# High products first, then low products, within each piece of a slab

## The reference

```
proj = x @ w_in                       # mixer layers, 2048 -> 4928
q = (rmsnorm(q_lat, q_norm_g) @ w_uq) ; kv = (rmsnorm(kv_lat, kv_norm_g) @ w_ukv)
y = pool_mixer(...) * silu(g_pool)    # small 128x128 products per group
out = mix @ w_out + b_out ; x = layernorm(DEEPNORM_ALPHA * x + out, ln_g, ln_b)
...
x = x + 0.5 * swiglu(rms_norm(x, ffn1_norm), ffn1_gate, ffn1_up, ffn1_down)   # 2048 -> 5632 -> 2048
proj = rms_norm(x, mix_norm) @ w_in ; x = x + mixed @ w_out
x = x + 0.5 * swiglu(rms_norm(x, ffn2_norm), ffn2_gate, ffn2_up, ffn2_down)
```

## Time and profile before

| | us |
|---|---|
| median of 3 runs | 2,604.45 |
| the profiled execution | 2,607.27 |
| its span | 2,605.5 |
| TensorE busy | 2,571.5 |
| VectorE busy | 1,784.4 |
| ScalarE busy | 1,360.1 |
| granted TensorE clock, mean | 0.998 |

### The profile page before, as it was taken

The page is one execution under the profiler, slowest core; times in us unless marked ns, Lnnn a source line. Parts: engine busy times, 40 slices in busy tenths (PEclk is TensorE's granted clock), DMA queues, the critical chain, the costliest instruction groups (busy, mean ns, idle before and its releaser), DMA issues.

```text
span 2605.5 us, 39929 instructions
## 1 busy us (share of the span) xinstructions
PE 2571.5 (99%) x14246; PEld 2221.6 (85%) x14246; DVE 1784.4 (68%) x2739; ACT 1360.1 (52%) x2112; POOL 0.2 (0%) x4
## 2 busy tenths in 40 slices
PE   7999999999999999999999999999999999999999
PEld 6888888888888888888888887887888888888888
DVE  8777657777658766556666765677776665666655
ACT  6665565565457444444445544774544444444443
POOL 0000000000000000000000000000000000000000
PEclk9999999999999999999999999999999999999999
DMA  7554555454554554565554653444455555555454
GB/s 281 196 184 170 186 210 222 152 187 164 182 209 167 200 184 179 183 202 192 190 193 158 198 210 137 149 152 148 177 195 190 193 168 191 205 193 187 172 186 164
DMA packets 75435, 482.41 MB, mean 185 GB/s; under 512 B 8384, under 2 KB 10816, under 8 KB 30784
## 3 DMA queue, kind: packets, MB, share of 16 engines
q1 hardware_dynamic: 75328, 480.99, 52.2%
HBM read 477.81 MB, written 2.10 MB: 184 GB/s over the span
## 4 chain that ended last, share of the span: by engine, by line
PE 82%; DVE 1%; ACT 1%; issue 0%; ACTq 0%; DVEq 0%
PE acc L800 46%; PE acc L801 23%; PE acc L806 3%; PE acc L808 3%; PE acc L807 3%; PE score L1063 1%; DVE low L1479 0%; PE head_ps L1086 0%; PE turn_ps L1072 0%; ACT high L1142 0%; PE score L800 0%; PE sums L1043 0%; PE head_ps L1087 0%; PE sums L1009 0%; ACT L1421 0%
## 5 line engine op out<-in xcount | busy, mean ns | idle before, releaser
L800 PE MATMUL acc<-xs,high 128*128 128x512 f32 x4096 | 1437.7, 397 | 3.5 <-DVE lat L1589 2.0
L1479 DVE TENSOR_TENSOR low<-raw,high 128x1024 fp32r<-128x1024 f32 (+2 forms) x976 | 1079.4, 1123 | 466.9 <-ACT high L1142 441.2
L1142 ACT ACTIVATE high<-raw 128x1024 fp32r<-128x1024 f32 (+2 forms) x976 | 946.3, 976 | 527.3 <-PE acc L801 382.9
L801 PE MATMUL acc<-xs,low 128*128 128x256 f32 x4096 | 1139.4, 278 | 0.0
L800 PEld LDWEIGHTS acc<-xs,high 128*128 128x128 f32 x4096 | 769.2, 188 | 185.0 <-DVE lat L1589 3.0
L801 PEld LDWEIGHTS acc<-xs,low 128*128 128x128 f32 x4096 | 770.9, 188 | 0.6
L800 PE MATMUL acc<-hidden,high 128*128 128x512 f32 x1408 | 488.9, 394 | 0.1
L1181 ACT ACTIVATE lowsum<-acc 128x256 f32<-128x256 f32 x356 | 136.0, 383 | 532.6 <-PE acc L801 532.3
L801 PE MATMUL acc<-hidden,low 128*128 128x256 f32 x1408 | 390.2, 277 | 0.0
L800 PEld LDWEIGHTS acc<-hidden,high 128*128 128x128 f32 x1408 | 264.0, 188 | 61.8 <-DVE low L1479 0.4
L801 PEld LDWEIGHTS acc<-hidden,low 128*128 128x128 f32 x1408 | 264.3, 188 | 0.0
(11 more groups left out here) (361 smaller groups left out, 1904.0 us busy)
## 6 DMA issues: line engine op xcount, KB each, us to landing
raw<-w_up_dram SPq DMA_DIRECT2D x176, 1024.0 KB, 4.8
raw<-w_down_dram SPq DMA_DIRECT2D x128, 704.0 KB, 4.1
raw<-w_in_dram SPq DMA_DIRECT2D x78, 1024.0 KB, 4.8
raw<-w_out_dram SPq DMA_DIRECT2D x32, 1024.0 KB, 4.8
raw<-w_heads_dram SPq DMA_DIRECT2D x24, 1024.0 KB, 4.8
raw<-w_mixout_dram SPq DMA_DIRECT2D x16, 1024.0 KB, 4.8
raw<-w_mem_dram SPq DMA_DIRECT2D x8, 1024.0 KB, 4.7
raw<-w_nat_dram SPq DMA_DIRECT2D x8, 1024.0 KB, 4.8
```

Of the source, the lines that this page charges most:

```text
L800: eng.matmul(bank_, hi, moving, start=start, stop=False)
L801: return eng.matmul(bank_[:, S:2 * S], lo, moving[:, 0:S], start=False, stop=stop)
L1142: eng.activation(high[:, s % SPLIT, to:to + n * P], raw[:, s % RAW, at_:at_ + n * P], ACT.Copy).then_inc((highs_a, highs_b)[piece], 1)
L1479: eng.tensor_tensor(low[:, s % SPLIT, w], raw[:, s % RAW, at_:at_ + n * P], high[:, s % SPLIT, w].bitcast(F32), ALU.subtract).then_inc((lo ...
```

## The change

In each piece of a slab the high products of all its blocks are issued first, then the low products of all its blocks; before, each block had its high and its low product in turn. The wait for the piece's low part stands before the first low product, and a new wait for its high part stands before the first high one. In the three regions that start with two tiles together (other than `mixout`), the order per block is high of tile 0, high of tile 1, low of tile 0, low of tile 1. In `mixout` it is by piece and tile. In `uq` and `uk` it is by output group (4 or 2 blocks).

The core of the diff:

```diff
-            def product(bank_, hi, lo, moving, start, stop):
+            def product_high(bank_, hi, moving, start):
 
                 eng.matmul(bank_, hi, moving, start=start, stop=False)
+
+            def product_low(bank_, lo, moving, stop):
+
                 return eng.matmul(bank_[:, S:2 * S], lo, moving[:, 0:S], start=False, stop=stop)
...
+                def piece_high(piece):
+
+                    eng.wait_ge((highs_a, highs_b)[piece], val(s + 1, 4, i))
...
+                    cuts = [(b, b + 1) for b in range(KT)] if r.name != "mixout" else [(0, 8), (8, KT)]
+                    for cut, n in [(cut, n) for cut in cuts for n in range(2)] if r.name == "mixout" else [(c, None) for c in cuts]:
+                        tiles = range(2) if n is None else (n,)
+                        for b in range(*cut):
...
+                            for m in tiles:
+                                product_high(banks[m], high[:, (s + m) % SPLIT, at_], in_mix(r)[:, b, :], b == 0)
+                        for b in range(*cut):
+                            at_ = slice(b * P, (b + 1) * P)
                             if b % 8 == 0:
+                                eng.wait_ge((lows_a, lows_b)[b // 8], s + tiles[-1] + 1)
+                            for m in tiles:
+                                last = product_low(banks[m], low[:, (s + m) % SPLIT, at_], in_mix(r)[:, b, :], b == KT - 1)
...
                 elif r.kind == "tile":
                     a = bank_free(k, 4)
-                    for b in range(KT):
-                        if b == 8:
+                    for piece in range(2):
+                        if piece:
                             for step in halfway:
                                 do(*step)
-                        if b % 8 == 0:
-                            piece_ready(b // 8)
-                        if k == 0 and split_norm(r.name):
-                            wait_split(eng, split_norm(r.name), b)
-                        last = product(a, *hl(b), in_mix(r)[:, b, :], b == 0, b == KT - 1)
-                        if b % 8 == 7:
-                            last.then_inc(products, 1)
+                        piece_high(piece)
+                        for b in range(8 * piece, 8 * piece + 8):
+                            if k == 0 and split_norm(r.name):
+                                wait_split(eng, split_norm(r.name), b)
+                            product_high(a, hl(b)[0], in_mix(r)[:, b, :], b == 0)
+                        piece_ready(piece)
+                        for b in range(8 * piece, 8 * piece + 8):
+                            last = product_low(a, hl(b)[1], in_mix(r)[:, b, :], b == KT - 1)
+                        last.then_inc(products, 1)
...
```

More of the change, by code:

```diff
@@ L861, in slot @@
                     banks = bank_free(0, 4), bank_free(1, 4)
[L862 to L874, removed]
-                            if b % 8 == 0:
-                                eng.wait_ge((lows_a, lows_b)[b // 8], s + n + 1)
-                        elif n == 0:
-                            wait_split(eng, split_norm(r.name), b)
-                            if b % 8 == 0:
[L880 to L887, removed]
-                            last.then_inc(products, 1)
@@ new lines, in slot @@
+                    cuts = [(b, b + 1) for b in range(KT)] if r.name != "mixout" else [(0, 8), (8, KT)]
[3 more added lines that the diff above has]
+                            at_ = slice(b * P, (b + 1) * P)
+                            if r.name == "in_a0" and b in (4, 8):
+                                turn_chunk("emb", b // 4 + 1)
+                            if r.name == "mixout":
+                                for step in steps if n == 0 else []:
+                                    if b == (LAST_TURNS[step[1] - MLA_ALL] if step[0] == "turn" else 8):
+                                        do(*step)
+                                if b % 4 == 0 and n == 0:
+                                    eng.wait_ge(mix_l, 4 * DEPTH + b // 4 + 1)
+                                if b % 8 == 0:
+                                    eng.wait_ge((highs_a, highs_b)[b // 8], s + n + 1)
+                            else:
+                                wait_split(eng, split_norm(r.name), b)
+                                if b % 8 == 0:
+                                    eng.wait_ge((highs_a, highs_b)[b // 8], s + 2)
+                            for m in tiles:
+                                product_high(banks[m], high[:, (s + m) % SPLIT, at_], in_mix(r)[:, b, :], b == 0)
+                        for b in range(*cut):
+                            at_ = slice(b * P, (b + 1) * P)
+                            if b % 8 == 0:
+                                eng.wait_ge((lows_a, lows_b)[b // 8], s + tiles[-1] + 1)
+                            for m in tiles:
+                                last = product_low(banks[m], low[:, (s + m) % SPLIT, at_], in_mix(r)[:, b, :], b == KT - 1)
+                                if m:
+                                    if b == KT - 1:
+                                        last.then_inc(products, 2)
+                                elif b % 8 == 7:
+                                    last.then_inc(products, 1)
@@ L906, in slot @@
                     a = bank_free(k // 2, 2) if not half else acc_of(r, r.t0 + k // 2)
[L907 to L913, removed]
+                    for piece in range(2):
+                        cut = (range(0, r.pieces[0]), range(r.pieces[0], HALF))[piece]
+                        piece_high(piece)
+                        for b in cut:
+                            product_high(a, hl(b)[0], hidden[:, HALF * half + b, :], half == 0 and b == 0)
+                        piece_ready(piece)
+                        for b in cut:
+                            last = product_low(a, hl(b)[1], hidden[:, HALF * half + b, :], half == 1 and b == HALF - 1)
+                        last.then_inc(products, 1)
                 elif r.kind in ("uq", "uk"):
@@ L919, in slot @@
                         a = bank_free(k * r.groups + m, 0)
+                        new = m * per in (0, r.pieces[0])
+                        if new:
+                            piece_high(int(m > 0))
                         for b in range(per):
-                            if m * per + b in (0, r.pieces[0]):
-                                piece_ready(int(m * per + b > 0))
-                            last = product(a, *hl(m * per + b), lats[:, src + b, :], b == 0, b == per - 1)
+                            product_high(a, hl(m * per + b)[0], lats[:, src + b, :], b == 0)
+                        if new:
+                            piece_ready(int(m > 0))
+                        for b in range(per):
+                            last = product_low(a, hl(m * per + b)[1], lats[:, src + b, :], b == per - 1)
                         last.then_inc(products, 1)
```

5 lines of the change are left out of this document (2 added, 3 removed).

## The result

The changed kernel takes 2,618.3 us in the median of four runs (2,616.4 to 2,619.9); the kernel before, run beside it, 2,603.75 (2,601.8 to 2,607.9). The medians lie 14.5 us apart; the ratio of the runs is 1.0049, with a 95% interval of 1.0035 to 1.0062, so it is slower by 9 to 16 us. The forecast was 2,598.5, and the time lies above the range's upper end of 2,614.

A forecast was written before the change was run, and what follows sets the result against it. TensorE's matmul pace was taken as the bound (busy 2,571.5 of 2,605.5 us). The terms 0 - 7 + 0.7 + 0.5 - 0.2 = -6.0 us gave 2,598.5 us for a median, range 2,587 to 2,614.

The forecast's parts named there:

- The failed step: Loops: low steps of 120 and high steps of 226.7 ns keep 346.7 a pair, so the change was put at nothing.
- the slower case: Rival: every high run starts unsettled, 3.8 ns a pair, 22 us, 2,628 us; decided by high steps above 227.9; chance 0.16.
- The sign: Loops: more than 581 matmuls in 100 us means shorter low runs, fewer than 575 an unsettled pace; either refutes it.
- The unrolled stretches: About 1,250 pairs at 353 ns regain nearly all of 6.3 ns, taken as 7 us less.
- Two tiles together: First tiles of both input projections and first feed-forward: tile 0's last low product 0.24 us later each, +0.7 us.
- The stop of mixout: Output projection of the mix: four low products now come behind TensorE's stop, 4 × 0.12 = +0.5 us.
- The waits: TensorE's wait on a low part goes, 0.2 us less; the two added waits a slab show no gap.

The follow-up runs named there:

- the feed-forward alone: The kernel before with the new order in `up` and `down` only, without the two tiles together; 2,615.9 us, ratio 1.0027.
- 512 columns in both products: Low product widened to all 512 columns, in the changed kernel (3,227.8 us) and in the kernel before (3,226.35 us), one run each.
- `mixout`'s start alone: The kernel before with the new order in the first two tiles of `mixout` only; 2,610.85 us, one run.
- the runs of eight in the unrolled regions: The kernel before with the new order in the unrolled tile regions only, `mixout`'s first two tiles left in turn; 2,607.1 us, ratio 0.9992.
- the waits of before: The changed kernel with one wait a piece, on the low part, ahead of its first high product; 2,620.8 us, ratio 1.0047.
- runs of four: The changed kernel with a piece's runs of eight cut into four high and four low products; 2,623.6 us, ratio 1.0059.
- of a slab: The changed kernel with one run over the whole slab, 16 high then 16 low products (11 and 11 in down); 2,613.5 us, ratio 1.0030.
- 384 columns: The changed kernel with low products of 384 columns, whose sums are not the reference's; 2,957.05 us, one run.
- runs of two: The changed kernel with a piece's runs of eight cut into two high and two low products; 2,608.4 us, ratio 1.0007.
- the unrolled regions alone: Two runs of the kernel before with the new order in the unrolled tile regions only: runs of eight (2,607.1 us) and of a slab (2,606.3 us).
- the first four experiments: Four follow-up experiments, not listed by name, beside which the kernel before had a median of 2,606.3 us.

## Why the prediction was wrong

**The failed step** is the sentence "I take the middle, 120 and 226.7, since both are the values at which a long run settles". That ends of the range stood beside it was right; the value taken was of the wrong kind. A run of eight is no long run. From low to high the pace starts as behind the transposes of the earlier trace rows, and it settles after five steps. The mean of the seven steps from high to high is (1,841 - 227) / 7 = 230.6, past the 227.9 from which, by the text, the slower case decides. For the piece that is 7 × 3.9 = 27 ns more; the step from high to low is 227 and not 231.5, 4.5 less; the low run with its step back is 952 and not 955.2. Together +20 ns, 2.5 a pair, where the step had 0. In the down projection it is 3.6. So the rival "slower: each change from low to high starts an unsettled run" was the mechanism, with its size of 3.8 ns put somewhat high, and with 0.16 it got too little. The argument against it, that the old order changes size all the time and its loops lose nothing, was no argument: with single steps between changes the pair has a cycle of its own (231.5 + 115.2), which says nothing of runs. What it costs: 4.5 + 0.8 + 5.9 us in the feed-forward, as against 0. The experiment with the feed-forward alone has the same, and those with 512 columns in both products show that it is the narrower low product, and not the grouping, that starts the unsettled run.

**The sign** named for it, fewer than 575 matmuls in 100 us, was just not met: there are 575, as 349.2 ns a pair gives. The full 3.8 ns would have given 572 or 573.

**The unrolled stretches** came out with the right sign. Pairs at 353.3 went to 349.2, 4.1 and not 6.3 ns, as they now have the unsettled runs too. 344 matmuls against 342 in the window instead of 346 or 347. The marks show -4.2 us up to 819 us and -0.8 from 1,804 to 1,887, where -7 was forecast for all such stretches; of the 4.2, 1.7 are a stretch at the lower clock that the kernel before had at 534 to 537 us and this execution hadn't. (The 20 us from 80 hold 115 matmuls in both; one matmul more would be 3 ns a pair there.) What is left is partly luck. The experiments with the feed-forward alone and with `mixout`'s start alone have the order of before up to 819 us, and by the same marks they stand at -0.2 and -1.0 there. In the second of them the pairs took 346.6 ns from 83 to 134 us, where the kernel before took 353.3, and it was the other way round from 1,450 to 1,540; before, then `mixout`'s start alone, with the same order there:

```profile
1450.00:1540.00 90.00, 90.00 (x521) 1.00 0.58 197
1450.00:1540.00 90.00, 90.00 (x512) 1.00 0.58 194
```

So the slow pattern doesn't belong to a stretch of the order: the same order, at a clock of 1.00, falls into it in one trace and not in the other. The 1,250 pairs of the forecast were those of one execution.

**Two tiles together** was right. The sequence after, at the end of `in_a0`, which answers to the earlier trace rows:

```profile
32.50 0.40 PE L804 MATMUL acc<-xs,low 128*128 128x256 f32 x2
32.82 0.38 ACT L1203 ACTIVATE lowsum<-acc 128x256 f32<-128x256 f32 x1 [2.49 <-PE acc L804]
33.23 0.42 DVE L1611 TENSOR_TENSOR lat<-acc,lowsum 128x256 f32<-128x256 f32 x1 [1.65 <-ACT lowsum L1203]
33.71 0.50 PE L800 MATMUL acc<-xs,high 128*128 128x512 f32 x1 [0.81 <-DVE lat L1611]
```

From the last low product to the next high one are 1,096 ns where before were 862; at the two sisters 1,090 for 861 and 1,093 for 866. That is 0.23 each, 0.24 was forecast.

**The stop of mixout** was sized at +0.5, and the place measured 2.7. The +0.5 for the four low products is right. Ahead of the stop 1.1 us more went to a longer stretch at the 1.2 GHz level; that isn't the order's doing, as the runs of eight in the unrolled regions, with the old order at this place, lost the same 1.1 there. Behind the stop the second stretch cost 1.5, and 0.4 came back up to 1,828 us. Left out was that work behind the stop may run at the 1.2 GHz level. Of the eight profiled kernels with the new order at this place six have the second fall (after, the waits of before, runs of four and of a slab, `mixout`'s start alone, 384 columns), and two haven't (runs of two, and the new order with 512 columns in both); of the six with the old order there none has it. What decides between them, the runs don't show.

**The waits** were right as to low parts: there is none on them, and with the old waits the time is the same.

**What stays open.** Why a change of the column count puts the next run out of step, whether it is the count or the half of the bank, and why a run of two loses less than one of four, no run shows; of the weight loads' cover, only what 175 ns would provide is ruled out. Nor does every such change do it: behind score products of 256 columns, at 1,642.6 us of the changed kernel, the second step of a run of 512 columns is 227 at once. And of the 14.5 us between the medians the two traces hold 9.1. Stretches at the 1.2 GHz level come and go between executions and kernels: in 520 to 545 the kernel before had a clock of 0.93 and 112 matmuls, after it 1.00 and 122; in 130 to 150 the clock was 1.00 in both and 0.91 in five of the experiments (the waits of before, runs of four and of two, and both with the unrolled regions alone). Each is worth 1.5 to 1.9 us, so two executions can lie some us apart with the same order. The mean clocks on record give an estimate of how much: at the 1.2 GHz level a step takes nearly twice as long (427 ns for 227), so a run loses up to its span times one minus its mean clock. The four runs of the changed kernel have 0.997, 0.995, 0.997 and 0.997, which makes 9 us; the 17 of the kernel before beside the first four experiments have 0.9984 in the mean, 4 us. So by this estimate some 5 of the 14.5 us are time at the lower clock, and the order's own part is some 9 or 10. Why the clock is lower more often in the changed kernel is open, beyond the second fall in `mixout`.

No version beat the kernel before: the two that touch the unrolled regions alone have intervals that include 1, and so has the one with runs of two.

## What to carry to other kernels

When an order is changed from alternating to grouped instructions, take the cost of a group from the first steps behind a change of shape as the trace shows them somewhere, not from the value that a long run settles at, and ask how many steps the group has. Where two sizes of matmul share the time, grouping them is no gain in itself: here single alternation, the odd-looking order, had the shortest pair in the loops of five run lengths. A stop that is followed by work at the lower clock costs more than its own length, so a change at a stop has a second possible price, what runs behind it. And before a gain is put on a slow stretch of one trace, see whether the stretch is slow in a second trace of the same order.

## What the runs showed of the hardware

- A high product behind a low one starts a run whose steps go 233, 236, 228, 233, 231 before the 227 of a settled run; behind 384 columns it doesn't settle within eight. With 512 columns in both products the loops show no such pattern in either order, 226 or 227 throughout.
- Low products of 256 columns behind high ones start 113 and 119 apart, then 120.
- One and the same alternating order ran at 346.7 ns a pair in one trace and at 353.4 in another, over the same 94 us and at a granted clock of 1.00.
- At the 1.2 GHz level the same steps are 427 and 214 ns. The Trainium skill (TensorE: Matmul & The Clock Gate, Part 1) has N ÷ 1.2 GHz for a cold array, 426.7 and 213.3: the trace agrees, there is no surplus over the columns. For the 2.4 GHz level the same part of the Trainium skill has N ÷ 2.4 GHz and some 2.5 ns, 215.7 for 512 columns: the trace doesn't agree, the best steps here are 226 to 227, so at this level each fp32 matmul with its own weights carries some 13 ns over its columns, and only at this level.
